# Three panels of the residual transposed by VectorE in 32 by 32 blocks instead of by TensorE, between layer 0's gate and layer 1's mixer

## The reference, cut to what matters

```python
        gate = jax.nn.sigmoid(h @ ple_w_gate[i] + ple_b_gate[i])
        h = h + gate * (p[i] @ ple_w_proj[i])
...
    for i in range(DEPTH):
        hn = rms_norm(h, ln_mix_pre[i])
...
            m = nsa_mixer(hn, cos128, sin128, nsa_w_in[j], ...)   # first step: hn @ nsa_w_in
```

## Time and profile before

| | |
|---|---|
| median of 3 runs | 2431.6 us (2429.13 to 2432.31) |
| the profiled execution | 2429.38 us, its span 2427.7 us |
| TensorE busy | 2398.8 us, 99% of the span |
| VectorE busy | 1499.5 us, 62% |
| ScalarE busy | 1047.4 us, 43% |
| granted TensorE clock, mean | 0.999 of full speed |

### The profile page before, as it was taken

The page is one execution under the profiler, slowest core; times in us unless marked ns, Lnnn a source line. Parts: engine busy times, 40 slices in busy tenths (PEclk is TensorE's granted clock), DMA queues, the critical chain, the costliest instruction groups (busy, mean ns, idle before and its releaser), DMA issues.

```text
span 2427.7 us, 29112 instructions
## 1 busy us (share of the span) xinstructions
PE 2398.8 (99%) x11640; PEld 2003.2 (83%) x11640; DVE 1499.5 (62%) x1572; ACT 1047.4 (43%) x1003; POOL 20.5 (1%) x38
## 2 busy tenths in 40 slices
PE   7999999999999999999999999999999999999999
PEld 7887888888888888888888888888888888888887
DVE  4654756666466655667676677566664667446675
ACT  5444445343333433345544355463343434334443
POOL 0000100000000000000000000000000000000000
PEclk9999999999999999999999999999999999999999
DMA  7554456665556556556555633465556665565564
GB/s 227 189 173 125 174 175 211 195 195 194 191 191 191 194 197 196 174 181 219 190 191 179 209 120 107 144 208 191 191 193 196 197 192 190 191 193 193 176 218 138
DMA packets 226967, 449.04 MB, mean 185 GB/s; under 512 B 7961, under 2 KB 19233, under 8 KB 225586
## 3 DMA queue, kind: packets, MB, share of 16 engines
q1 hardware_dynamic: 225218, 440.72, 55.5%
q10 hardware_dynamic: 1648, 6.89, 0.8%
HBM read 445.48 MB, written 2.10 MB: 184 GB/s over the span
## 4 chain that ended last, share of the span: by engine, by line
PE 97%; DVE 2%; ACT 1%; issue 0%; DMA 0%; ACTq 0%; DVEq 0%
PE PG L546 89%; PE MB L546 1%; PE MB L877 1%; PE MB L669 1%; PE MB L649 1%; PE MB L679 0%; ACT whl L1048 0%; DVE whl L1472 0%; PE MB L647 0%; PE MB L651 0%; PE MB L688 0%; PE PG L590 0%; PE PG L591 0%; PE PG L592 0%; PE MB L614 0%
## 5 line engine op out<-in xcount | busy, mean ns | idle before, releaser
L1472 DVE TENSOR_TENSOR whl<-raw,whl 128x2048 fp32r<-128x2048 f32 (+4 forms) x435 | 955.8, 2198 | 762.5 <-ACT whl L1048 762.2
L1048 ACT ACTIVATE whl<-raw 128x2048 fp32r<-128x2048 f32 (+4 forms) x435 | 800.8, 1841 | 1167.0 <-PE PG L546 1151.1
L546 PE MATMUL PG<-whl,XBh 128*128 128x512 f32 (+1 forms) x3376 | 796.6, 386 | 0.9 <-DVE whl L1472 0.5
L546 PE MATMUL PG<-whl,XAh 128*128 128x512 f32 (+1 forms) x3136 | 741.9, 387 | 2.2 <-ACT whl L1048 2.2
L546 PEld LDWEIGHTS PG<-whl,XBh 128*128 128x128 f32 x3376 | 624.9, 188 | 127.5 <-DVE whl L1472 0.9
L546 PEld LDWEIGHTS PG<-whl,XAh 128*128 128x128 f32 x3136 | 584.1, 188 | 119.1 <-ACT whl L1048 3.0
L546 PE MATMUL PG<-whl,XBl 128*128 128x512 f32 (+1 forms) x1688 | 412.5, 386 | 0.0
L546 PE MATMUL PG<-whl,XAl 128*128 128x512 f32 (+1 forms) x1568 | 383.4, 386 | 0.0
L546 PEld LDWEIGHTS PG<-whl,XBl 128*128 128x128 f32 x1688 | 313.1, 188 | 63.2
L546 PEld LDWEIGHTS PG<-whl,XAl 128*128 128x128 f32 x1568 | 291.9, 188 | 57.1
L2036 DVE STREAM_TRANSPOSE HT<-Hb 32x256 f32<-32x256 f32 x352 | 153.4, 436 | 5.6
(11 more groups left out here) (341 smaller groups left out, 1007.0 us busy)
## 6 DMA issues: line engine op xcount, KB each, us to landing
raw<-in_ffn_w_gate SPq DMA_DIRECT2D x88, 1024.0 KB, 5.2
raw<-in_ffn_w_up SPq DMA_DIRECT2D x88, 1024.0 KB, 5.2
raw<-in_ffn_w_down SPq DMA_DIRECT2D x64, 1024.0 KB, 5.0
raw<-in_nsa_w_in SPq DMA_DIRECT2D x36, 1024.0 KB, 5.1
raw<-in_ple_w_gate SPq DMA_DIRECT2D x32, 1024.0 KB, 5.1
raw<-in_ab_w_in SPq DMA_DIRECT2D x24, 1024.0 KB, 5.3
raw<-in_ffn_w_down SPq DMA_DIRECT2D x32, 768.0 KB, 4.3
raw<-in_ab_w_out SPq DMA_DIRECT2D x16, 1024.0 KB, 5.3
```

The lines of the kernel that those rows point to most:

```text
L546: return mm(bank(m), X[x][:, chunk, m * P:(m + 1) * P], w[:, k, c * ncol:(c + 1) * ncol], start=x == 0 and w is wh and c == 0 and pos in ( ...
L1048: A(wh[:, place % 2, 0:w], raw[:, place, 0:w], ACT.Copy).then_inc(hi_ready, 1)
L1472: V.tensor_tensor(wl[:, k, 0:w], raw[:, place, 0:w], wh[:, k, 0:w].bitcast(F32), ALU.subtract).then_inc(lo_ready, 1)
```

## The change

For panels 0, 1 and 2, `fresh_in` no longer runs on TensorE. In its place VectorE transposes the panel of `h` into a new buffer `XT` (which takes the place of `Hb` in memory) in 16 instructions, in four groups of four: `turn(i, 0)` after `gate_mul` and the slot's second split, `turn(i, 1)` after the third split, `turn(i, 2)` and `turn(i, 3)` after the fourth. ScalarE's four copies and VectorE's four subtractions then read `XT` instead of `MB`, and ScalarE's wait for `tx_ps` is now on VectorE. Panel 3 is handled as before.

```diff
+        XT = zt("XT", 36864, [P, 4, SEQ])
...
-                        if j == 1:
-                            fresh_in(q, s - GATE[0] - 1, panel_here)
+                        if (s, j) == (L1, 1):
+                            fresh_in(q, 3, panel_here)
...
-                    split_in(XIN[1][0], 2, TQ["mix1"], 0, 32, 2 * i, 4)
+                    if i < 3:
+                        act.wait_ge(tx_ps, TQ["mix1"] + 2 * i + 2)
+                        for c in range(4):
+                            k = 4 * i + c
+                            last = A(XIN[1][0][:, k, :], XT[:, c, :], ACT.Copy, scale=vcol[:, 32 + k:33 + k])
+                            if c % 2:
+                                last.then_inc(tx_hi, 1)
+                    else:
+                        split_in(XIN[1][0], 2, TQ["mix1"], 0, 32, 2 * i, 4)
...
+                def turn(i, a):
+                    v.wait_ge(h_ok, i + 1)
+                    v.wait_ge(tx_lo, TQ["mix1"] + 2 * i)
+                    r = slice(32 * a, 32 * a + 32)
+                    src = h[r, :, 512 * i:512 * i + 512].rearrange("p m (c q i) -> p c m q i", c=4, q=4)
+                    for q in range(4):
+                        dst = XT[32 * q:32 * q + 32, :, :].rearrange("p c (m a j) -> p c m a j", m=2, a=4)
+                        last = V.transpose(dst[:, :, :, a, :], src[:, :, :, q, :])
+                    return last
...
+                        if j and i < 3:
+                            turn(i, j - 1)
-                    split_in(XIN[1], 2, TQ["mix1"], 0, 32, 2 * i, 4)
+                    if i < 3:
+                        turn(i, 3).then_inc(tx_ps, 2)
+                        for c in range(4):
+                            k = 4 * i + c
+                            v.wait_ge(tx_hi, TQ["mix1"] + 2 * i + c // 2 + 1)
+                            last = V.scalar_tensor_tensor(XIN[1][1][:, k, :], XT[:, c, :], vcol[:, 32 + k:33 + k],
+                                                          XIN[1][0][:, k, :].bitcast(F32), ALU.mult, ALU.subtract)
+                            if c % 2:
+                                last.then_inc(tx_lo, 1)
+                    else:
+                        split_in(XIN[1], 2, TQ["mix1"], 0, 32, 2 * i, 4)
```

## The result

The changed kernel takes 2438.46 us (median of 7 runs, 2436.82 to 2440.4), the kernel before 2431.6 us. The ratio is 1.0034 with a 95% interval of 1.0024 to 1.0044, so it is slower by 0.34%, some 8 us by the ratio and 6.9 by the medians. The forecast was 2437.0 us with slower as the likeliest case: right in sign and mechanism, and short in size. The profiled execution took 2440.24 us with a mean granted clock of 0.997.

A forecast was written before the change was run, and what follows sets the result against it. TensorE, busy 99% of the span, was taken as the bound. Panel slots of +1.2, +2.0 and +2.0 us, removed transposes included, plus 0.15 gave +5.4 us on 2431.6: 2437.0 us, range 2434.0 to 2441.5.

The forecast's parts named there:

- TensorE's saving, -2.8 us: Panels 0 to 2: removing eight transposes with changeovers takes three times 0.93 us off TensorE's path.
- VectorE's price: VectorE's 16 transposes a panel take 436 ns each, one starting every 0.448 us: 7.2 us a panel.
- the sum in the prediction: Slots of panels 1 and 2: VectorE's splits, gate work and transposes run without pause for 19.95 us.
- The second rival: Every panel costs what panel 0 does: +3.7 us in all, 2435.3 us; chance 0.17.
- Panel 0, +1.2 us: Panel 0's slot: TensorE waits 2.1 us for ScalarE's split; slot 23.85 us instead of 22.69, removed transposes included.
- Panels 1 and 2, +2.0 each: Slots of panels 1 and 2: the VectorE and ScalarE loop, 24.7 us, sets their length; TensorE waits 2.8 us.
- Behind the last wait, +0.15 us: TensorE's first eight matmuls after a wait take 1.96 us instead of 1.81; this counts once, behind the last wait.
- The sum, +5.4 us: Whole kernel: 1.2 + 2.0 + 2.0 + 0.15 = 5.35 us, on 2431.6 us giving 2437.0, 0.22% slower.
- The clock: Rival: clock falls to 1.2 GHz for one unit behind each new wait, 3 x 5.4 us more, 2453; chance 0.02.
- The cover: ScalarE's next split is done 3.2 us before TensorE needs it; rival that this holds: 2428.8 us, chance 0.06.
- The advice of the Trainium skill: Rule against the change: TensorE for whole 128 by 128 transposes where PSUM will do, VectorE for 32 by 32.
- What the profile was to show: TensorE waits of 2.1, then twice 2.8 us; no VectorE pause over 0.2 us for panels 1 and 2; 436 ns transposes.

The follow-up runs named there:

- Split first: Changed kernel, but ScalarE makes the high part of the next slot's first unit before it waits for VectorE's transposes; 2428.8 us, ratio 0.9989 to the kernel before.
- filled wait: Changed kernel plus 16 identity transposes on TensorE at the end of each of the three gate slots; 2436.9 us, ratio 1.0026 to the kernel before.
- before the fourth: Changed kernel, but VectorE makes its last eight transposes ahead of its split of the fourth unit; 2428.53 us, ratio 0.9995 to the kernel before.
- one-panel kernel: Changed kernel, but only panel 0 is transposed by VectorE, panels 1 and 2 by TensorE; 2434.55 us, ratio 1.0011 to the kernel before.
- fewer transposes: Changed kernel with the third group of four transposes left out for panels 1 and 2; 2432.79 us, ratio 1.0011 to the kernel before.

## Why the prediction was right, and where it was short

- **TensorE's saving, -2.8 us: right.** Split first, which has the saving and no wait, gains 2.6 us in the stretch and 0.11% in the timing.
- **VectorE's price: right.** The transposes out of `h` take 436 ns on average, as those out of `Hb`. In panel 2's slot VectorE runs from 1181.50 to 1201.45 without a pause, 19.95 us, which is the sum in the prediction. The second rival (every panel costs what panel 0 does) is out: the later slots are dearer, 24.9 and 25.0 against 24.1.
- **Panel 0, +1.2 us: measured +1.4.** **Panels 1 and 2, +2.0 each: measured +2.2 and +2.3** with the clock at 1.00. Both are short by the same two terms of the chain. From ScalarE's first copy to its next split it is 1153.81 - 1150.84 = 2.97 us, where I took 2.77 and 0.04 more from copies out of PSUM. And TensorE starts 0.13 us after the split ends, where I took 0.05.
- **Behind the last wait, +0.15 us: measured +0.1** (11.01 us instead of 10.89 in the filled wait).
- **The sum, +5.4 us: +6.1** for the chain alone; the other 2.4 of the profiled stretch's 8.5 are the clock.
- **The clock: the step that was mis-sized.** I gave it 2 in 100 and let it cost a whole unit behind each wait, 16 us together. It does fall, but not behind each wait, and costs 1.6 us a time. In panel 1's slot most of a fall is hidden, since VectorE's chain sets that slot's length and not TensorE: the slot is 25.75 us, 0.8 longer than with the clock held. Behind the last wait nothing hides it. My evidence against it, one wait of 2.25 us that left the clock at 1.00, was no evidence. The trace's first record of the granted clock begins 18.1 us into the span, and the view counts what no record covers as 1.00. The durations say otherwise: the eight matmuls behind that wait took 2.82 us, the next eight of their kind 1.60.

```profile
15.00 2.82 PE L546 MATMUL PG<-whl,XAh 128*128 128x368 f32 x8 [2.25 <-ACT whl L1048]
...
18.66 1.60 PE L546 MATMUL PG<-whl,XAl 128*128 128x368 f32 x8
```

  The Trainium skill, TensorE: Matmul & The Clock Gate, Part 1, says that an idle TensorE goes back to half its rate and, of the change up to the full rate, that its moment varies from run to run. These traces agree with the first (granted clock 0.87 behind two of the three waits), and they show the same scatter on the way down: behind one and the same wait of 1.54 us the clock fell in five of nine profiles. The rule deserved more than a chance of 0.02.
- **The cover.** The prediction had the last transpose of panel 0 due 16.9 us after the slot's start and coming at 19.0. It came at 19.0, behind 3.59 us of transposes, and TensorE waited. In the kernel before the fourth it came at 16.4, and the first wait was gone. Where between 16.4 and 19.0 the point lies, no run shows.
- **The advice of the Trainium skill** (VectorE: DVE Perf Modes, Rules for kernel authors) to leave whole tiles to TensorE fits the cost in engine time, 7.2 us against 0.93 a panel. It does not decide the time here: split first follows the change and is 0.11% faster, because VectorE had the 7.2 us to spare.
- **What the profile was to show.** The waits were forecast as 2.1, 2.8, 2.8 and are 2.13, 2.13, 2.97; the second is short because TensorE, slowed by the clock, was late itself, and VectorE paused 0.87 us for it. `gate_mul` starts 25.1, 25.7 and 24.9 us apart, where 24 to 25 was forecast.

Why the clock fell behind the first and the third wait and not behind the second stays open. It is not the length of the wait alone: the same 2.14 us was followed by a fall in one kernel and by none in another, and the same 1.54 us both ways. No run here varies the length of a wait by itself.

## What to carry to other kernels

When work moves from the engine that bounds the kernel to one with time to spare, don't ask whether the time is there, but when the last piece ends and what is queued behind the instruction that waits for it. Here an in-order queue put the next split of ScalarE behind a wait for VectorE, and a gain of 2.6 us became a loss of 8.5 in the profiled stretch (6.1 with the clock held); moving one line ahead of the wait gives the gain. Take the chain from the last transpose to TensorE's next start link by link: each link that was moved, shortened or reordered showed in the length of its slot to within 0.4 us of what the chain gave.

## What the runs showed of the hardware

- TensorE's granted clock can fall behind a wait of about 2 us, and need not, after 900 us in which TensorE was never idle for as much as 1 us. A wait of 2.14 us was followed by a granted clock below full in the one-panel kernel (the first 8 matmuls took 3.21 us) and by full clock in the kernel with fewer transposes (2.08). A fall costs 1.6 us where nothing hides it.
- A shorter wait can be enough: behind the 1.54 us at 86 us of the program the clock fell in five of the nine profiles. Behind the waits of 0.39 to 1.61 us in the changed stretch (ten of them, four kernels) it stayed at its full 2.4 GHz.
- With idle work in the wait, 16 transposes of 128 by 128 in 1.91 us, the clock stayed at 1.00 behind all three waits, and at 0.999 or more on average in each of nine runs.
- Four copies of 128 by 256 with a scale for each row take 1.71 us out of SBUF and 1.55 out of PSUM on ScalarE.
